# The first modulation totals in PSUM, and half of the first normalized tiles and k-steps ahead of the last weights

## The reference

```
c_act = silu(c)
mod = c_act @ ada_w[layer] + ada_b[layer]          # 1024 -> 6 * 1024
sh1, sc1, g1, sh2, sc2, g2 = split(mod, 6)
h = rmsnorm(x, norm_g[layer, 0]) * (1 + sc1) + sh1
q, k, v = split(h @ da_w_in, 3)                    # layer 0
...
x = x + g1 * y
```

## Time and profile before

| | |
|---|---|
| median of 3 runs | 1470.75 us (1466.32 to 1472.23) |
| profiled execution, its span | 1463.8 us |
| the profiled execution's own time beside the span | not given; the median is 6.95 us over the span |
| PE busy | 1286.9 us (88%) |
| DVE busy | 1063.8 us (73%) |
| ACT busy | 572.8 us (39%) |
| POOL busy | 590.2 us (40%) |

### The profile page before, as it was taken

The page is one execution under the profiler, slowest core; times in us unless marked ns, Lnnn a source line. Parts: engine busy times, 40 slices in busy tenths (PEclk is TensorE's granted clock), DMA queues, the critical chain, the costliest instruction groups (busy, mean ns, idle before and its releaser), DMA issues.

```text
span 1463.8 us, 17111 instructions
## 1 busy us (share of the span) xinstructions
PE 1286.9 (88%) x5478; PEld 999.1 (68%) x5478; DVE 1063.8 (73%) x1310; ACT 572.8 (39%) x871; POOL 590.2 (40%) x273
## 2 busy tenths in 40 slices
PE   4988899889799889999999675776999999999996
PEld 2666677666677677788887453443768888887885
DVE  5577776755888998886347999999458898896002
ACT  3455545544423333342223432443445435442121
POOL 1323322232423342454442675665224545545340
PEclk8899999999899989999999897788999999999998
DMA  8523333222434454224442101000122232233221
GB/s 327 190 101 129 115 134 124 87 89 85 159 128 143 144 169 138 94 95 152 169 158 87 58 29 58 29 29 29 43 73 86 86 114 86 93 106 106 92 87 61
DMA packets 44917, 156.76 MB, mean 107 GB/s; under 512 B 4936, under 2 KB 5192, under 8 KB 44880
## 3 DMA queue, kind: packets, MB, share of 16 engines
q1 hardware_dynamic: 43488, 153.98, 30.8%
q10 hardware_dynamic: 1392, 2.32, 0.6%
HBM read 154.15 MB, written 2.12 MB: 107 GB/s over the span
## 4 chain that ended last, share of the span: by engine, by line
PE 57%; DVE 29%; issue 7%; ACT 4%; DMA 2%; DVEq 0%; SPq 0%; ACTq 0%
PE psum L823 18%; PE psum L825 17%; PE psum L824 17%; DVE acc_a L1547 6%; DVE acc_b L1547 6%; DVE acc_mid L1172 2%; DVE z L1293 2%; DMA ada_first<-ada_w 2%; DVE tmp L1442 2%; PE psum L834 2%; DVE tmp L1214 1%; ACT L555 1%; DVE h_lo L1218 1%; DVE pt_lo L1302 1%; DVE acc L1172 1%
## 5 line engine op out<-in xcount | busy, mean ns | idle before, releaser
L453 POOL TENSOR_TENSOR w_lo<-w_raw,w_hi 128x1024 fp32r<-128x1024 f32 (+1 forms) x192 | 485.3, 2543 | 760.2 <-ACT w_hi L534 760.2
L823 PE MATMUL psum<-h_hi,w_hi 128*128 128x512 f32 x1152 | 477.7, 415 | 15.1 <-DVE h_lo L1218 7.9
L825 PE MATMUL psum<-h_hi,w_lo 128*128 128x512 f32 x1152 | 459.2, 399 | 0.0
L824 PE MATMUL psum<-h_lo,w_hi 128*128 128x512 f32 x1152 | 458.7, 398 | 0.0
L823 PEld LDWEIGHTS psum<-h_hi,w_hi 128*128 128x128 f32 x1152 | 223.6, 194 | 71.4 <-issue 12.7
L824 PEld LDWEIGHTS psum<-h_lo,w_hi 128*128 128x128 f32 x1152 | 223.4, 194 | 48.5 <-issue 5.3
L825 PEld LDWEIGHTS psum<-h_hi,w_lo 128*128 128x128 f32 x1152 | 222.1, 193 | 48.4
L534 ACT ACTIVATE w_hi<-w_raw 128x1024 fp32r<-128x1024 f32 (+1 forms) x192 | 191.7, 1037 | 82.0 <-DMA w_raw<-w_tiles 81.8
L1400 DVE SCALAR_TENSOR_TENSOR x<-psum,mod,x 128x512 f32<-128x512 f32 (+1 forms) x32 | 23.3, 749 | 182.2 <-PE psum L825 182.2
L823 PE MATMUL psum<-a_hi,w_hi 128*128 128x512 f32 x352 | 139.3, 396 | 0.7 <-issue 0.7
L825 PE MATMUL psum<-a_hi,w_lo 128*128 128x512 f32 x352 | 138.9, 395 | 0.0
(11 more groups left out here) (175 smaller groups left out, 1651.9 us busy)
## 6 DMA issues: line engine op xcount, KB each, us to landing
w_raw<-w_tiles SPq DMA_DIRECT2D x160, 512.0 KB, 3.3
ada_buf<-ada_w SPq DMA_DIRECT2D x32, 512.0 KB, 3.3
ada_mid<-ada_w SPq DMA_DIRECT2D x32, 512.0 KB, 3.4
w_raw<-w_tiles SPq DMA_DIRECT2D x32, 448.0 KB, 3.1
ada_first<-ada_w SPq DMA_DIRECT2D x16, 512.0 KB, 6.0
ada_late<-ada_w SPq DMA_DIRECT2D x16, 512.0 KB, 4.2
x<-x_in SPq DMA_DIRECT2D x4, 512.0 KB, 9.9
bias<-rel_scratch ACTq DMA_DIRECT2D x1, 2048.0 KB, 8.3
```

The lines of the kernel that those rows point to most:

```text
L453: nc.gpsimd.tensor_tensor(w_lo[:, slot, 0:k], w_raw[:, (ph.tile + l) % 2, 0:k], f(w_hi[:, slot, 0:k]), ALU.subtract).then_inc(lo_done, 1)
L823: nc.tensor.matmul(dst, w_hi[:, slot, k], rhs_hi, start=first, stop=False)
L824: nc.tensor.matmul(dst, w_hi[:, slot, k], rhs_lo, start=False, stop=False)
L825: return nc.tensor.matmul(dst, w_lo[:, slot, k], rhs_hi, start=False, stop=last)
```

## The change

Five things change in the code.

- The two running totals of a chunk stand in PSUM banks 2 and 6 (`FIRST_ACC`); only the chunk's last two products write to the SBUF totals that PE reads.
- DVE computes the first four normalized tiles behind the second piece of chunk 2, ahead of the chunk's other two pieces and all of chunk 3.
- PE runs `first_ada` for chunks 0 and 1 first, then 30 turns of `keep_warm` on bank 1, then the query and key products of k-steps 0 to 3, and behind k-step 3 `first_ada` for chunks 2 and 3.
- The table's second product goes to bank 0 instead of bank 6, and PE waits for `pt_read` ahead of the query product.
- DVE waits ahead of each chunk's first products as well (`ada_used`), since the totals' banks are used again.

```diff
@@ -215,6 +215,8 @@
         lam_p = at("lam_p", [P, 2, HD], F32, o_at + 64 + 4 * RELS_PAD + 16 * HD)
 
         first_sums = ((acc[:], v_t[:]), (v_even[:], v_odd[:]))
+        FIRST_ACC = (2, 6)
+        EARLY_WARM, REST_OF_TAB = 1, 0
         ada_first = at("ada_first", [P, 4, 2, S], F32, qk_base)
 
 
@@ -546,7 +548,7 @@
             act.wait_ge(pt_done, 1)
             nc.scalar.activation(rel_rows[:, 0:S], psum[0:HEADS, PT, :], ACT.Copy).then_inc(pt_read, 1)
             act.wait_ge(pt_done, 2)
-            nc.scalar.activation(rel_rows[:, S:RELS_PAD], psum[0:HEADS, PT + 1, 0:RELS_PAD - S], ACT.Copy)\
+            nc.scalar.activation(rel_rows[:, S:RELS_PAD], psum[0:HEADS, REST_OF_TAB, 0:RELS_PAD - S], ACT.Copy)\
               .then_inc(pt_read, 1)
             act.wait_ge(pt_read, 2)
             act.dma_start(scratch, rel_rows[:]).then_inc(rel_out, 16)
@@ -838,7 +840,7 @@
 
             pe.wait_ge(consts_in, 64)
             nc.tensor.matmul(psum[0:HEADS, PT, :], tab[:], onehot[:, 0:S], start=True, stop=True).then_inc(pt_done, 1)
-            nc.tensor.matmul(psum[0:HEADS, PT + 1, 0:RELS_PAD - S], tab[:], onehot[:, S:RELS_PAD],
+            nc.tensor.matmul(psum[0:HEADS, REST_OF_TAB, 0:RELS_PAD - S], tab[:], onehot[:, S:RELS_PAD],
                              start=True, stop=True).then_inc(pt_done, 1)
 
             def square_sum(n, last):
@@ -851,11 +853,11 @@
                     nc.tensor.matmul(psum[:, OB], ones[:], tmps[m % 2][:], start=False,
                                      stop=(m == DK - 1)).then_inc(sq_added, 1)
 
-            def keep_warm(n):
+            def keep_warm(n, bank=WARM):
 
 
                 with pe.Fori(0, n):
-                    nc.tensor.matmul(psum[:, WARM, 0:P], ones[:], ones[:], start=True, stop=True)
+                    nc.tensor.matmul(psum[:, bank, 0:P], ones[:], ones[:], start=True, stop=True)
 
             def first_ada(ch):
                 pe.wait_ge(ada_used, 8 * (ch + 1))
@@ -874,8 +876,10 @@
                 pe.wait_ge(sq_ready, m + 1)
                 nc.tensor.matmul(psum[:, OB], ones[:], tmps[m % 2][:], start=(m == 0),
                                  stop=(m == DK - 1)).then_inc(sq_added, 1)
-            for ch in range(CH0):
+            for ch in range(2):
                 first_ada(ch)
+            keep_warm(30, EARLY_WARM)
+            pe.wait_ge(pt_read, 2)
 
             def head_products(it, c, steps, base=0):
 
@@ -964,6 +968,7 @@
                         10: (lambda: turn_p(3),), 12: (output,), 14: (ada,), 15: (mean_square,)}
 
             beside = {DK + k: (lambda h=k: turn_bias(h),) for k in range(DK)}
+            beside[DK // 2 - 1] = tuple(lambda ch=ch: first_ada(ch) for ch in range(2, CH0))
             head_products(0, 0, beside)
             with pe.Fori(0, 3) as it:
                 head_products(it, 0, attention_steps(it, 0), base=1)
@@ -1172,21 +1177,23 @@
                     V.scalar_tensor_tensor(out=total, in0=buf, scalar=scalar, in1=total,
                                            op0=ALU.mult, op1=ALU.add).then_inc(ada_used, 1)
 
-            def first_chunk(ch):
-                for n in range(4):
+            def first_chunk(ch, first=0, end=4):
+                for n in range(first, end):
                     p = 4 * ch + n
                     dve.wait_ge(ada_first_landed[p % 4], 16 * (p // 4 + 1))
                     for kk in range(2):
-                        k, total = 2 * n + kk, first_sums[ch % 2][kk]
+                        k, total, running = 2 * n + kk, first_sums[ch % 2][kk], psum[:, FIRST_ACC[kk]]
                         if k == 0 and ch >= 2:
                             dve.wait_ge(ada_mm, ch - 1)
+                        if p:
+                            dve.wait_ge(ada_used, 2 * p + kk - 1)
                         if n == 0:
-                            V.tensor_scalar(total, ada_first[:, p % 4, kk], cact[:, k:k + 1], None, ALU.mult)\
+                            V.tensor_scalar(running, ada_first[:, p % 4, kk], cact[:, k:k + 1], None, ALU.mult)\
                              .then_inc(ada_used, 1)
                         else:
-                            dve.wait_ge(ada_used, 2 * p + kk - 1)
-                            V.scalar_tensor_tensor(out=total, in0=ada_first[:, p % 4, kk], scalar=cact[:, k:k + 1],
-                                                   in1=total, op0=ALU.mult, op1=ALU.add).then_inc(ada_used, 1)
+                            V.scalar_tensor_tensor(out=total if n == 3 else running, in0=ada_first[:, p % 4, kk],
+                                                   scalar=cact[:, k:k + 1], in1=running,
+                                                   op0=ALU.mult, op1=ALU.add).then_inc(ada_used, 1)
 
             def first_out(ch):
 
@@ -1225,14 +1232,15 @@
             first_chunk(0)
             lambda_sums()
             first_chunk(1)
-            first_chunk(2)
+            first_chunk(2, 0, 2)
             first_out(0)
             first_out(1)
             dve.wait_ge(sc_read, 2)
             gain_of(0, 0, DK // 2)
-            first_chunk(3)
             dve.wait_ge(rms_ready, 1)
             norm_tiles(0, 0, DK // 2)
+            first_chunk(2, 2)
+            first_chunk(3)
             first_out(2)
             first_out(3)
             dve.wait_ge(sc_read, 4)
```

## The result

The changed kernel takes 1477.02 us (median of 5 runs, 1476.25 to 1480.18) against 1470.75 (1466.21 to 1472.23): ratio 1.0057, 95% interval 1.0036 to 1.0077. It is slower by 6.3 us between the medians; I had forecast 3.7. (The two medians alone give 1.0043, which lies in the interval.) Timed a second time, unedited, it came out at 1.0038 (1.0023 to 1.0052).

What follows compares the result with a forecast made beforehand. TensorE, 88% busy, runs without a stop once head 0's query and key products start; the steps ahead put their end at 62.15 instead of 58.45, so 1470.75 + 3.7 = 1474.5 us, range 1467.5 to 1479.

Steps and rivals of the forecast that it cites:

- the landing of piece 15: Last piece of modulation weights: issued at 41.3, landing at 47.3, between 44.6 and 48.3, with half the bias load's 2.0 us.
- the clock of the last ones-products: TensorE's ones-products of chunk 3, no longer covered by the tiles: 1.8 us at full clock, 3.6 as upper bound.
- piece 9's products beside GpSimd: Second piece of chunk 2 on VectorE: running operand in PSUM, so unheld, 27.30 to 28.63, under 0.8 us a product.
- gain product: VectorE, chunk 2's stretch: starts at about 29.1 with both operands in SBUF, getting in between GpSimd's two residuals.
- first tile's product: First normalized tile on VectorE: held behind GpSimd's second residual, ending at 33.54 instead of 42.66, 9.1 us earlier.
- its products end (T): End of piece 15's two VectorE products, 1.4 us after it lands: 48.7, not under 46.3 by VectorE's own work.
- gain product done: Second gain product on VectorE, after chunk 3's totals: held by GpSimd's residual from 50.1 to 52.5.
- k-steps 4 to 7: TensorE's later query and key products: 5.55 us at full clock plus 1.8 for 3.8 us of half clock.
- mark, by the difference: Shift of the end of head 0's query and key products, 62.15 against 58.45: 3.7 us later, carried through to the end.
- My rival in which they are held too: Products on PSUM do not escape GpSimd's hold: first tile ends near 33.8, 0.3 us beyond forecast, 1474.8 us; chance 0.06.
- The rival of an earlier mark: Shorter wait for piece 15, T at 46.3 and clock holding: marker at 56.5, 1.9 us earlier, 1468.8 us; chance 0.28.
- Both upper bounds: Piece 15 at 48.3 and chunk 3's ones-products at half clock: 2.0 us beyond forecast, 1476.5 to 1479 us; chance 0.12.

Runs made afterwards that it cites:

- the new order: The new order and added keep_warm, with running totals left in SBUF, against the kernel before: ratio 1.0052, mark 66.32 us; the changed kernel's mark is 64.99.
- the old order: Totals in PSUM alone, with VectorE and TensorE order of the kernel before and no added keep_warm: ratio 0.9985, 1467.30 us, mark 56.39.
- chunk 2 whole: Changed kernel with all four pieces of chunk 2 ahead of the four tiles: 1.0010; the same with keep_warm(9) behind the last ones-products: 0.9983.
- the bias load late: Changed kernel with the 2 MB bias load issued behind the split of head 0's value weights: ratio 1.0025, mark 64.09 us.
- the filled gaps: Changed kernel with keep_warm(14) between the ones-products of chunks 2 and 3 and keep_warm(8) behind them: ratio 1.0043, mark 64.63 us.
- the second pair: Changed kernel and kernel before, both run again unedited: medians 1474.38 against 1468.15 us, ratio 1.0038, marks 64.87 and 58.81.

## Why the prediction was right and wrong

The direction held, and the chain of steps in the main; the size did not. Two terms of the sum failed, the landing of piece 15 and the clock of the last ones-products. With them the 0.88 for a change within 0.5% was misplaced: the first comparison's ratio, 1.0057, is just over that bound, while the second's, 1.0038, is under it. The two intervals overlap from 1.0036 to 1.0052.

| step | forecast | measured | second execution |
|---|---|---|---|
| piece 9's products beside GpSimd | unheld | unheld (1.40 for two) | the same |
| gain product | from 29.1, between the residuals | 30.53 to 32.80, held | 29.37 to 31.63, held |
| first tile's product | held, ends 33.54 | not held, ends 33.58 | not held, ends 32.4 |
| fourth tile complete | 38.6 | 38.65 | 37.48 |
| piece 15 issued, landed | 41.3, 47.3 | 41.3, 49.05 | 40.15, 47.96 |
| its products end (T) | 48.7 | 50.5 | 49.4 |
| last ones-products | 1.8 us, full clock | 3.6 us, half clock | 3.6 us, half clock |
| gain product done | 52.5, held | 54.7, not held | 53.6, not held |
| fifth tile complete | 54.8 | 57.04 | 55.94 |
| k-steps 4 to 7 | 7.35 us | 7.3 us | 8.2 us |
| mark, by the difference | +3.7 | +5.86 | +6.06 |

**Totals in PSUM.** Right that the hold is handed on rather than removed, and wrong on who bears it: the forecast had the gain product slip in between the two residuals and the first tile stand behind the second. In both executions the gain product stood behind the second itself and the tile ran unheld; in the first it also came 1.4 us late, 0.97 of it a wait for TensorE's ones-products of chunk 1, which ran at half clock (3.6 us). That the first tile ended where I had it (33.58 for 33.54) is because either way is released by the end of GpSimd's pair. By the Trainium skill, "SBUF — State Buffer", section "Who interferes with whom", a VectorE instruction with two inputs in SBUF contends with a GpSimd instruction that reads SBUF; the trace agrees, 2.27 for the gain product beside 1.40 for two products with a total in PSUM. My rival in which they are held too is out. Right too that the first product of a chunk loses its pace: the second starts 0.66 after the first (1.40 for both), where one took 0.48. I had called the PSUM part next to nothing (0.3 in the new order); the runs give 1.3 there, and 2.7 in the old order.

**Pieces 14 and 15.** The term "I take 47.3, with half the cost" was mis-sized. It had 5.0 us for the piece and 1.0 for the bias load. Piece 15 landed 7.7 us after its issue (7.8 in the second execution), above even my upper bound of 7.0, at 48.3: without the bias load beside it it took 5.6 and 5.2, and the load cost it about 2 us, the whole cost and not half. Issued early (chunk 2 whole), 5.4 us of the mark come back. So the four products moved behind the tiles, which SyncE waits for, are shown as the cost. The bias load has about 2 us of the delay.

**The ones-products.** The term "I take 1.8" was wrong, and it was a choice: the clock fell near 47.0, some 2.5 us after the last wide product, and near 47.9, 4.3 us after it, in the second execution. The late piece is not what did it: with the bias load late the totals were ready at 48.6, as forecast, and the ones-products took 3.6 us as well. This costs 1.8. It also took the gain product past GpSimd's residual, so the 1.5 of hold that I had added were not paid. These two nearly cancel, and the filled gaps showed both: the faster ones-products ran into the hold.

**K-steps 4 to 7** were right in cause, half clock for their first part. The size was met by luck: the half clock lasted 3.5 us in the first execution and 5.5 in the second, against the 3.8 that I had taken from one place before.

**The rivals.** The rival of an earlier mark needed T under 48.2 with the full clock; T was 50.5, and with the bias load late it was 48.6, with the clock at half. "Both upper bounds" (2.0 beyond the forecast) is what happened, by 2.2; it had 0.12.

**The end.** That the shift carries through one for one is borne out by the second pair's totals and by the medians of both comparisons. What the chances gave too little to (0.08 to slower) is that the case at 1476.5, with medians that scatter by several microseconds, stands close enough under the bound (1478.1) to cross it.

## What to carry to other kernels

A queue that waits for a consumer's count makes each instruction moved ahead of that consumer a delay of the transfers behind it: four products moved behind four tiles put two loads off by 5.7 us, and they then met another load. Ask of a reordering not what starts earlier but what is issued later. Where VectorE's operands in SBUF are held behind GpSimd, putting one in PSUM is worth trying alone; what it frees should not be given to the next instruction whose tensors all stand in SBUF.

## What the runs showed that was not expected

The clock's return did not follow the start of the wide products. With products from 55.26 it came back at about 60.8, with products from 57.09 at about 60.6: 5.5 and 3.5 us. An earlier start bought half of its 1.8 us there. The edit isn't what decides this: the changed kernel itself, run again, started them at 56.00 and had the clock back at about 61.5. So a single execution's mark can hide a gain of 1 us, or show one that isn't there. And the loop that nobody reads went with a full clock in one kernel (1.00 from 44 to 60 us), while in another it fell at about 53.8 with the loop running, and in a third (chunk 2 whole) it stayed at half through all 3.8 us of the loop; what decides between them stays open.

The split of the best kernel's gain stays open too: 0.9966 for the totals in PSUM with keep_warm against 0.9985 without, with a mark that differs by 0.16 us. The profiled execution doesn't show what the loop gave.
